# A convolution's channel sum taken over by VectorE, and four modulation pieces placed before the last pair of chunks

## The reference

```python
def conv_module(h, w_pw1, w_dw, b_dw, ln_g, ln_b, w_pw2):
    u = h @ w_pw1
    a, gate = jnp.split(u, 2, axis=-1)
    u = a * jax.nn.sigmoid(gate)
    u = lax.conv_general_dilated(
        u, w_dw[:, None, :].astype(u.dtype), window_strides=(1,),
        padding=[(CONV_PAD, CONV_PAD)], dimension_numbers=('NWC', 'WIO', 'NWC'),
        feature_group_count=D_MODEL) + b_dw
    u = jax.nn.silu(layer_norm(u, ln_g, ln_b))
    return u @ w_pw2
```

## Time and profile before

| What | us |
|---|---|
| Median of 3 runs | 1512.65 |
| Lowest, highest | 1510.72, 1512.73 |
| The profiled execution's own time | 1512.73 |
| Its span in the trace | 1510.9 |
| PE busy | 1434.8 (95%) |
| DVE busy | 945.1 (63%) |
| ACT busy | 584.9 (39%) |
| POOL busy | 390.5 (26%) |

### The profile page before, as it was taken

How to read it: one execution, slowest core, us unless ns; L and a number is a source line. 1 busy time by engine, 2 the same in 40 slices (tenths; PEclk the granted TensorE clock), 3 DMA queues, 4 the chain that set the end, 5 groups by cost and what they waited for, 6 DMA issues and landing times.

```text
span 1510.9 us, 24508 instructions
## 1 busy us (share of the span) xinstructions
PE 1434.8 (95%) x10544; PEld 1246.0 (82%) x10544; DVE 945.1 (63%) x1127; ACT 584.9 (39%) x704; POOL 390.5 (26%) x302
## 2 busy tenths in 40 slices
PE   5888999989999999999899999999999998899999
PEld 5887899979999997764477888888886965899998
DVE  7877665466768666866637777256415578586343
ACT  5623445443334364210624222332223457433433
POOL 4975603000003400000002343442330010034553
PEclk9999999989999999999899999999999999999999
DMA  8532324555666465975426655334333400475552
GB/s 264 170 119 90 113 88 144 202 181 190 228 226 234 168 223 179 256 217 139 149 77 218 207 168 167 126 128 163 115 111 112 167 29 2 140 223 170 193 171 82
DMA packets 159540, 239.64 MB, mean 159 GB/s; under 512 B 6960, under 2 KB 129872, under 8 KB 159312
## 3 DMA queue, kind: packets, MB, share of 16 engines
q1 hardware_dynamic: 154640, 233.11, 47.2%
q10 hardware_dynamic: 4800, 5.08, 1.4%
HBM read 227.55 MB, written 1.05 MB: 151 GB/s over the span
## 4 chain that ended last, share of the span: by engine, by line
PE 85%; DVE 8%; ACT 3%; issue 2%; DMA 1%; SPq 0%; POOL 0%; DVEq 0%; ACTq 0%; POOLq 0%
PE bank L2087 25%; PE bank L2088 25%; PE bank L2089 25%; PE bank L2397 2%; DVE wlo L1144 1%; PE bank L2151 1%; PE bank L2565 1%; ACT whi L681 1%; PE bank L2554 1%; PE bank L2239 1%; DVE stat L1826 1%; PE bank L2276 1%; DVE A L1297 1%; PE bank L609 1%; PE bank L590 1%
## 5 line engine op out<-in xcount | busy, mean ns | idle before, releaser
L2087 PE MATMUL bank<-ahi,whi 128*128 128x256 f32 (+1 forms) x2480 | 795.2, 321 | 29.0 <-POOL alo L625 7.6
L2088 PE MATMUL bank<-alo,whi 128*128 128x256 f32 (+1 forms) x2480 | 786.4, 317 | 0.0
L2089 PE MATMUL bank<-ahi,wlo 128*128 128x256 f32 (+1 forms) x2480 | 785.9, 317 | 0.0
L681 ACT ACTIVATE whi<-raw 128x2048 fp32r<-128x2048 f32 x160 | 306.3, 1915 | 720.1 <-PE bank L2089 720.1
L1144 DVE TENSOR_TENSOR wlo<-raw,whi 128x2048 fp32r<-128x2048 f32 x160 | 367.1, 2295 | 346.6 <-ACT whi L681 346.2
L2087 PEld LDWEIGHTS bank<-ahi,whi 128*128 128x128 f32 x2480 | 480.0, 194 | 73.0 <-issue 33.5
L2089 PEld LDWEIGHTS bank<-ahi,wlo 128*128 128x128 f32 x2480 | 479.9, 194 | 28.9
L2088 PEld LDWEIGHTS bank<-alo,whi 128*128 128x128 f32 x2480 | 480.4, 194 | 27.7 <-issue 0.2
L2054 POOL TENSOR_TENSOR A<-A 128x512 f32 (+1 forms) x48 | 106.8, 2238 | 482.8 <-ACT A L1010 482.8
L2036 POOL TENSOR_TENSOR alo<-A,ahi 128x512 fp32r<-128x512 f32 (+1 forms) x43 | 126.5, 2945 | 353.8 <-ACT ahi L884 353.8
L1508 DVE SCALAR_TENSOR_TENSOR A<-modraw,scc,A 128x1024 f32<-128x1024 f32 x70 | 121.3, 1772 | 0.6
(11 more groups left out here) (301 smaller groups left out, 1195.2 us busy)
## 6 DMA issues: line engine op xcount, KB each, us to landing
raw<-in_w_ff SPq DMA_DIRECT2D x64, 1024.0 KB, 5.2
modraw<-in_w_mod SPq DMA_DIRECT2D x72, 512.0 KB, 4.5
raw<-in_w_in SPq DMA_DIRECT2D x28, 1024.0 KB, 5.2
A<-in_w_mod SPq DMA_DIRECT2D x24, 512.0 KB, 4.7
raw<-in_pw SPq DMA_DIRECT2D x12, 1024.0 KB, 7.4
raw<-in_w_ffn_gate SPq DMA_DIRECT2D x11, 1024.0 KB, 5.3
raw<-in_w_ffn_up SPq DMA_DIRECT2D x11, 1024.0 KB, 5.3
raw<-in_w_ffn_down SPq DMA_DIRECT2D x11, 1024.0 KB, 5.2
```

The lines of the kernel that those rows point to most:

```text
L681: act.activation(whi[:, k % 2, :], raw[:, kk, :], ACT.Copy).then_inc(whi_ready, 1)
L2087: pe.matmul(out_, w_hi, a_hi, start=start, stop=False, **kw)
L2088: pe.matmul(out_, w_hi, a_lo, start=False, stop=False, **kw)
L2089: return pe.matmul(out_, w_lo, a_hi, start=False, stop=stop, **kw)
```

## The change

On DVE, each finished chunk is added to a running sum `csum` of 128 by 512 (chunk 0 and 1 make the first sum; six additions in all, the last after chunk 6). On PE, seven of the eight channel sums go; `seven_sum` multiplies `csum` by the matrix of ones, and one `channel_sum(7)` follows. Pieces 34 and 35 are taken right behind 32 and 33, ahead of `convolve(6)`. On DVE, `store_mods` of row 2 and 3 moves behind the reciprocal, and PE waits for it before it turns row 4. On ACT, one small activation with the root function is put behind the last pair's copies.

```diff
+        csum = area(9984, 512)
@@ ACT
             each_block(act, "pw1", act_pw1, roll=False)
+            act.activation(stat[:, 50:51], epsb, ACT.Sqrt)
@@ DVE
+            def chunk_added(c):
+
+                if c == 0:
+                    return
+                dve.wait_ge(conv_out, c + 1)
+                if c >= 2:
+                    dve.wait_ge(chunks_added, c - 1)
+                dve.tensor_tensor(csum, cacc[:, 0, :, :].rearrange("p s t -> p (s t)") if c == 1 else csum,
+                                  cacc[:, c, :, :].rearrange("p s t -> p (s t)"), ALU.add).then_inc(chunks_added, 1)
@@
                         convolved(p.least - 5)
                         convolved(p.least - 4)
+                        chunk_added(p.least - 5)
+                        chunk_added(p.least - 4)
@@
             convolved(5)
+            chunk_added(4)
+            chunk_added(5)
             taps_of(3, 6, VTAPS)
             convolved(6)
+            chunk_added(6)
             convolved(7)
-            store_mods(0, 4, 2, 2, 7)
-
             dve.wait_ge(msum_done, 1)
...
             dve.reciprocal(rstd[:, 0:128], rstd[:, 0:128]).then_inc(lrstd_ready, 1)
+            store_mods(0, 4, 2, 2, 7)
             dve.wait_ge(lspread_done, 1)
@@ PE
+            def seven_sum():
+                pe.wait_ge(chunks_added, KD - 2)
+                pe.matmul(pb[0][:, :], C["ones"], csum, start=True, stop=False)
+
             def channel_sum(c):
                 pe.wait_ge(conv_out, c + 1)
-                return pe.matmul(pb[0][:, :], C["ones"], cacc[:, c, :, :], start=(c == 0), stop=(c == KD - 1))
+                return pe.matmul(pb[0][:, :], C["ones"], cacc[:, c, :, :], start=False, stop=True)
@@
             convolve(4)
-            pe.wait_ge(u_ready, KD)
-            for c in range(2):
-                channel_sum(c)
             convolve(5)
-            for c in range(2, 5):
-                channel_sum(c)
             mod_turn(3)
-            mod_pieces(32, 2)
-            channel_sum(5)
+            mod_pieces(32, 4)
             convolve(6)
             convolve(7)
-            channel_sum(6)
-            mod_pieces(34, 2)
+            pe.wait_ge(u_ready, KD)
+            seven_sum()
             channel_sum(7).then_inc(msum_done, 1)
@@
                 if l == 1:
+                    pe.wait_ge(mod_ready, 2)
                     mod_turn(4)
```

More of the change, by code:

```diff
@@ L324, in program @@
         conv_out = sem("conv_out")
+        chunks_added = sem("conv_chunks_added")
         msum_done = sem("mean_done")
```

## The result

The changed kernel takes 1514.69 us (median of 16 runs, 1513.52 to 1518.98) against 1512.55 (16 runs, 1510.48 to 1514.24). The ratio is 1.0017, with a 95% interval of 1.0011 to 1.0024: slower by 2.6 us (1.7 to 3.6). The forecast was +3.3 us, 1516.0, the range 1512.6 to 1518.2. The most likely of the three classes was "slower by over 0.2%" with 0.50; the measured ratio lies just inside 0.2%, in the class that had 0.44.

What follows compares the result with a forecast made beforehand. PE held 85% of the chain, and the last copies were taken to bound `convolve(6)` and `convolve(7)`. Wait +3.8, clock +1.8, tail -1.0 and root's table -1.3 made +3.3 us on 1512.73: 1516.0, range 1512.6 to 1518.2.

Steps and rivals of the forecast that it cites:

- The wait for pieces 34 and 35: On PE ahead of `convolve(6)`: their late loads make it start at 717.1 instead of 713.28, +3.8 us.
- The clock: TensorE falls to 1.2 GHz in the long idle before `convolve(6)` and `convolve(7)`, which then need +1.8 us more.
- The tail: On PE behind `convolve(7)`: two sums and no pieces before the mean's subtraction, 2.13 instead of 3.15 us, -1.0 us.
- The root's table: On ACT in the norm: the table load before the root leaves the chain, -1.28 us.
- The additions and `store_mods`: On DVE: six additions hidden in idle or unawaited, and the store moved into a wait behind the reciprocal, 0 us.
- Clock up: Rival: TensorE stays at 2.4 GHz through the idle before `convolve(6)`; +1.1 us, 1513.8, chance 0.13.
- Pieces in time: Rival: pieces 34 and 35 land no later than the last copy; 1510.4, or 1512.7 with clock down; chance 0.12.
- Down for the whole pair: Rival: `convolve(6)` and `convolve(7)` run wholly at half clock, twice 8.79 us; 1523.0, chance 0.06.

Runs made afterwards that it cites:

- e1: Changed kernel with pieces 34 and 35 taken behind the last channel sum; 1512.16 us against 1512.46 for the kernel before.
- e2: Changed kernel with SP's loads of pieces 34 and 35 issued ahead of its last pair's copies; 1510.41 us against 1512.46 for the kernel before.
- e8: Changed kernel with twelve unneeded matmuls on PE between pieces 33 and 34; 1515.27 us against 1511.96 for the kernel before.
- e4: Kernel before with only pieces 34 and 35 moved ahead of `convolve(6)`, all eight sums kept on PE; 1516.47 us against 1512.46.
- e5: Changed kernel with eight unneeded matmuls on PE between pieces 33 and 34; 1516.07 us against 1512.33 before, profiled again at 1516.5.
- e3: Kernel before with only the small root activation added behind the last pair's copies; 1511.48 us against 1512.46.
- e10: Kernel before with only the six additions on DVE, their sum unread and PE's eight sums kept; 1511.35 us against 1511.96.
- e9: Kernel before with only pieces 34 and 35 moved behind the eighth channel sum; 1511.36 us against 1511.96.
- e6: Changed kernel with eight unneeded matmuls ahead of `convolve(6)` and pieces 34 and 35 behind the last channel sum; 1508.16 us against 1512.33 before.

## Why the prediction was right, and where not

- **The wait for pieces 34 and 35** was the largest term, +3.8; the changed kernel's trace shows +4.1, within the bounds of 2.9 to 4.5, and 4.6 against the other kernels, just above them. The times of e1, e2 and e8 put it at 4.3 to 5.0. The mechanism is as predicted, and the term was somewhat small. Piece 35 took 1.08 us, the end of my range and not the 0.9 that I took; its load landed 6.7 us after its issue and not 6.2.
- **The clock** was put at +1.8. The profile has +1.3 and e1 and e2 1.8 to 1.9. The bounds of 1.2 to 2.6 hold all three, but the sum behind the 1.8 has a gap: of the 4.6 us of work at 1.2 GHz it took off piece 35 and left out piece 34. In the changed kernel PE did 4.59 us of work before the clock rose, and both pieces, 1.08 us each, were part of it; 2.42 were left for the pair. In e1 and e2 it was 3.8 us, all in the pair. And I took a long idle for the cause, and in e4 a shorter one for safe; e4 and e5 show otherwise. The trace of before had it: two of its three stretches "after short waits", from 569.36 and 579.60, came 1.3 to 1.8 us behind the end of waits of 1.82 and 2.02 us. Where the clock fell early in a long idle, part of the low stretch was spent in the idle (4.96 us of 10.2 before piece 34 in the changed kernel); where it fell late, behind a shorter wait, most of it was paid in the pair (e4). That `convolve` slows in full proportion, my assumption, holds: with 2.42 us at half clock in the pair the loss is 1.2 to 1.3.
- **The tail**: -1.0 predicted, -1.2 in the trace.
- **The root's table** was mis-sized: -1.3 in the sum, -0.5 in the trace of the change and -0.8 in e3. I read the load of 1.28 us in the chain as wholly in series. The chain names only what ended last; beside the load ran PE's sum of the last squares, and once the load is gone the root waits for that sum. I had the row for it (in the later norm the root waits 0.55 us for PE behind the squares) and used it only to show that no table comes in between. No row bears out the drain of the Trainium skill (ScalarE: Activation LUTs, section "What ACT_TABLE_LOAD costs"): the early load in the changed kernel takes the same 1.28 us, and removing it from the chain gave 0.5 to 0.8, not 2.66.
- **The additions and `store_mods`** at nothing: they cost nothing, by the trace of the change and by e10. That the additions let the last product on DVE start 0.36 us sooner I had not foreseen.
- **The total.** With 4.1 + 1.3 - 1.2 - 0.5 the profile gives +3.7, with the 0.36 on DVE +3.4; sixteen runs give +2.6. That the sum of +3.3 came so near is in part luck: against this profile the wait was put 0.3 too low and the root's gain 0.8 too high, and against these stand 0.5 too much for the clock, 0.2 too little gain from the tail and the 0.36 left out. Part of the difference between +3.4 and +2.6 may lie in what I compared with. I took the kernel before as one whose pair runs at full clock, as in its profile. In some executions it may not, as e9 shows behind the same work; the sum should have carried a share of that on the side of before. How large it is over many executions was not measured, and the profile of the changed kernel is one execution of sixteen too.
- **The rivals.** "Clock up" falls by all six profiles with a wait of 2.6 us or more ahead of the pair. "Pieces in time" needed an order that SP does not have; with that order made (e2) the time was 1510.41, beside the 1510.4 that this rival gave with the clock up; but here the clock was down, for which it gave 1512.7, so that this agreement is chance. "Down for the whole pair" never came: 11.24 us was the longest.

What stays open: how often the clock falls behind a short wait, before and in the variants, and for how long, was not counted; why the additions let DVE's product start sooner is not shown; why e8, its pair at full clock, is no faster than the changed kernel is not either; and the 13.9 us of the kernel before against 13.2 to 13.5 elsewhere rests on one profile.

## What to carry to other kernels

Work moved ahead of a wait on the critical engine must have its own data by then: look at the landing of each transfer it needs, not at when it was used before, since a use that never waited says nothing of how early it could be. Before taking hidden work off TensorE, ask what it fills: an idle in front of work on the critical path can cost that work part of its clock, whether it is long or short. Filling it in part was no help here (e5 against the changed kernel); filling it to its end took 2.2 us off where nothing else was waited for (e6 against e1), and nothing that the times show where a load still was (e8 against the changed kernel). When a step is taken out of the chain, look for what ran beside it, as that is the new bound. And one profile of each side is one execution of each: compare a term with more than one kernel that has it.

## What the runs showed of the hardware

A shorter idle was no protection for TensorE's clock. It fell at the end of a wait of 1.40 us (e9), in the second of two waits of 2.70 and 1.08 or 2.58 and 1.62 with a piece between (e5), and in that of 3.13 and 1.03 (e4); in other executions it stayed up through 1.1 to 1.8 us. The stretch at 1.2 GHz was 3.4 us in one execution and 6.8 in another of the same kernel, at the same place, which moved the pair from 9.77 to 11.22 us. By the Trainium skill (TensorE: Matmul & The Clock Gate, section "HAM oscillation — how this bites in real kernels") a wait for a DMA between bursts lets the clock fall, and the next burst begins cold. The traces agree in that the clock fell in or right behind each wait of over 2.5 us on a `w_mod` load ahead of the pair. They agree with the cold start only in the changed kernel, where piece 34 took 1.08 us behind 9.04 us of idle; in e4 and e5 it took 0.64 us behind 2.6 to 3.1, at 2.4 GHz, and the clock fell behind it.
